# Residual kept token-major: activations stationary, 512 weight columns streamed per load in the FFNs and output projections

## What is computed

```python
for i in range(4):                     # first model; mixers: gated delta, stick-breaking, sparse, gated delta
    x = x + 0.5 * swiglu(rmsnorm(x, ffn1_norm[i]), w_gu, w_down)        # 1024 -> 2 x 2816 -> 1024
    x = x + mixer(rmsnorm(x, mix_norm[i]))                              # ends in h @ w_out, 1024 x 1024
    x = x + 0.5 * swiglu(rmsnorm(x, ffn2_norm[i]), w_gu, w_down)
x = rmsnorm(x, final_norm)
# second model, with gate, shift and scale per feature from a modulation vector
xs + 0.5 * gate * swiglu_2(rmsnorm(xs, g) * (1 + scale) + shift, w_gate, w_up, w_down)   # ctx once, x four times
x + gate * attention(...) ; x + gate * conv(...)                        # one each, both end in @ w_out
rmsnorm(x, final_g)

def rmsnorm(x, g): return x * rsqrt(mean(x * x, -1) + eps) * g
def swiglu(h, ...): return (silu(h @ gate) * (h @ up)) @ down
```

## Time and profile before

| | us |
|---|---|
| median of three runs | 3996.16 |
| range of the runs | 3991.67 to 3997.68 |
| the profiled execution, span | 3996.0 |
| TensorE busy | 3679.5 (92%) |
| VectorE busy | 2434.3 (61%) |
| ScalarE busy | 1783.3 (45%) |
| GpSimd busy | 559.9 (14%) |
| mean granted TensorE clock | 0.954 |

### The profile page before, as it was taken

How to read it: one execution, slowest core, us unless ns; L and a number is a source line. 1 busy time by engine, 2 the same in 40 slices (tenths; PEclk the granted TensorE clock), 3 DMA queues, 4 the chain that set the end, 5 groups by cost and what they waited for, 6 DMA issues and landing times. The chain is left out here.

```text
span 3996.0 us, 67990 instructions
## 1 busy us (share of the span) xinstructions
PE 3679.5 (92%) x28562; PEld 3552.6 (89%) x28562; DVE 2434.3 (61%) x2565; ACT 1783.3 (45%) x2047; POOL 559.9 (14%) x208
## 2 busy tenths in 40 slices
PE   7998788999899998699999789899999889999999
PEld 7997688999899997599999689899999669999999
DVE  4575459797577776677777545554546544545644
ACT  3353255665355554355555234344443344444343
POOL 0001126462032330133310110000001000000000
PEclk9998798999999999899999899999999899999999
DMA  5542045565366663275744015445444215454453
GB/s 206 180 153 79 1 169 210 215 228 200 109 241 235 230 238 115 94 265 211 262 179 169 1 43 190 158 170 178 170 177 166 83 44 194 154 193 158 158 179 126
DMA packets 89670, 652.27 MB, mean 163 GB/s; under 512 B 10000, under 2 KB 10000, under 8 KB 10640
## 3 DMA queue, kind: packets, MB, share of 16 engines
q1 hardware_dynamic: 78480, 572.05, 39.3%
q0 software_dynamic: 11008, 77.60, 5.4%
HBM read 648.56 MB, written 1.05 MB: 163 GB/s over the span
## 5 line engine op out<-in xcount | busy, mean ns | idle before, releaser
L1348 DVE TENSOR_TENSOR w_lo<-raw,w_hi 128x2048 fp32r<-128x2048 f32 x540 | 1390.0, 2580 | 890.0 <-ACT w_hi L909 889.9
L498 PE MATMUL wrk<-h_hi,w_hi 128*128 128x256 f32 x5748 | 1649.5, 287 | 112.7 <-DVE h_lo L1360 68.2
L499 PE MATMUL wrk<-h_hi,w_lo 128*128 128x256 f32 x5748 | 1642.1, 286 | 0.0
L500 PE MATMUL wrk<-h_lo,w_hi 128*128 128x256 f32 x5748 | 1641.2, 286 | 0.0
L909 ACT ACTIVATE w_hi<-raw 128x2048 fp32r<-128x2048 f32 x540 | 1029.9, 1911 | 1047.1 <-PE wrk L500 975.1
L498 PEld LDWEIGHTS wrk<-h_hi,w_hi 128*128 128x128 f32 x5748 | 1120.0, 195 | 125.0 <-issue 118.9
L499 PEld LDWEIGHTS wrk<-h_hi,w_lo 128*128 128x128 f32 x5748 | 1120.3, 195 | 0.4 <-issue 0.2
L500 PEld LDWEIGHTS wrk<-h_lo,w_hi 128*128 128x128 f32 x5748 | 1119.4, 195 | 0.0
L498 PE MATMUL acc<-hid_hi,w_hi 128*128 128x256 f32 x2288 | 652.1, 285 | 21.3 <-DVE w_lo L1348 21.1
L499 PE MATMUL acc<-hid_hi,w_lo 128*128 128x256 f32 x2288 | 650.2, 284 | 0.0
L500 PE MATMUL acc<-hid_lo,w_hi 128*128 128x256 f32 x2288 | 650.1, 284 | 0.0
(11 more groups left out here) (244 smaller groups left out, 3065.5 us busy)
## 6 DMA issues: line engine op xcount, KB each, us to landing
raw<-in_wts SPq DMA_DIRECT2D x540, 1024.0 KB, 4.8
arena<-in_mods POOLq DMA_DIRECT2D x72, 1024.0 KB, 5.1
const<-in_const SPq DMA_DIRECT2D x1, 2176.0 KB, 10.0
c<-in_bias POOLq DMA_DIRECT2D x8, 256.0 KB, 2.9
x<-in_x SPq DMA_DIRECT2D x1, 1024.0 KB, 5.3
c<-in_c SPq DMA_DIRECT2D x1, 1024.0 KB, 5.1
out<-x SPq DMA_DIRECT2D x1, 1024.0 KB, 3.9
vec<-in_vec SPq DMA_DIRECT2D x1, 402.5 KB, 3.2
```

The costliest lines, as they stand in the source:

```text
L498: nc.tensor.matmul(o, wh, rh, start=first, stop=False, skip_group_check=True)
L499: nc.tensor.matmul(o, wl, rh, start=False, stop=False, skip_group_check=True)
L500: return nc.tensor.matmul(o, wh, rl, start=False, stop=last, skip_group_check=True)
L1348: tt(w_lo[:, ns % SLOTS, :], raw[:, ns % SLOTS, :], w_hi[:, ns % SLOTS, :].bitcast(F32), ALU.subtract).then_inc(lo_ready, 1)
```

## The change

The residual becomes token-major (`x`: two halves of 128 tokens on the partitions, 1024 features on the free axis), and so do the results of the FFNs and of the output projections. In those, the activations are now the stationary operand (128 features x 128 tokens) and 512 columns of weights are streamed, which fill a bank. A piece of gate and up holds 512 feature rows of both, 256 columns each. `across` and `along` of the mixers' other projections stay.

- The mean of squares is now a sum along the free axis: ScalarE squares with an accumulator (`statistics`), no matmuls.
- The matmuls still need features on the partitions. TensorE transposes x (16 transposes of 128 x 128 per norm, into `acc`), ScalarE scales and rounds to `h_hi` (`turned_high`), VectorE takes the difference (`turned_low`); with a shift it is two operations per chunk. In a late FFN x is turned unnormalised, and `rstd` is a column that goes into the Silu and into the product.
- `hid` comes out token-major, so each step transposes it (four transposes) before it is split.
- Where the next operation is a late FFN (`follower`), two of its four groups of transposes stand between the last matmuls of the operation before.
- The gate of the second model was a column per partition; it is now a row. Seven operations build it with eight small matmuls (`gate_rows`) and multiply with it in an operation of its own.
- Output projections take the inner dimension in halves, the FFN order on TensorE is rewritten, the loops are unrolled, and the closing norms' gains are loaded as rows.

```diff
+                def gate_up(s, p, t):
+                    n = ns + (3 * s - 1 if s else 0) + p
+                    pe.wait_ge(lo_ready, n + 1)
+                    if s == 0:
+                        pe.wait_ge(n_lo_ready, turned_bank(i, t, p))
+                    u = use[name, f"gu{s}{t}"]
+                    o = bank(u) if p == 0 else wrk[:, u % BANKS, :]
+                    for q in range(4):
+                        k, w = 4 * p + q, slice(q * NB, (q + 1) * NB)
+                        m = products(o, h_hi[:, k, tok(t)], h_lo[:, k, tok(t)], w_hi[:, n % SLOTS, w], w_lo[:, n % SLOTS, w], k == 0, k == KC - 1)
...
+                def turn_hid(s):
+                    pe.wait_ge(taken, use[name, f"gu{s}1"] + 1)
+                    o = bank(use[name, f"t{s}"])
+                    for j in range(2):
+                        for t in range(2):
+                            m = nc.tensor.transpose(o[:, j * T + t * P:j * T + (t + 1) * P], hid[:, t, j * P:(j + 1) * P], cst("ident"))
...
+                def down(s, t, half):
+                    n, q = ns + (3 * s + 4 if s < STEPS - 1 else 3 * s + 2), s % 2
+                    pe.wait_ge(lo_ready, n + 1)
+                    pe.wait_ge(taken, use[name, f"t{s}"] + 1)
+                    for j in range(2):
+                        w = slice(j * D + half * NB, j * D + (half + 1) * NB)
+                        m = products(acc[:, 2 * t + half, :], hid_hi[:, q, j, tok(t)], hid_lo[:, q, j, tok(t)],
+                                     w_hi[:, n % SLOTS, w], w_lo[:, n % SLOTS, w], s == 0 and j == 0, s == STEPS - 1 and j == 1)
...
+                for s in range(1, STEPS):
+                    gate_up(s, 0, 0)
+                    gate_up(s, 0, 1)
+                    turn_hid(s - 1)
+                    gate_up(s, 1, 0)
+                    gate_up(s, 1, 1)
+                    down(s - 1, 0, 0)
+                    down(s - 1, 0, 1)
+                    if s == STEPS - 1:
+                        turn_hid(s)
+                    down(s - 1, 1, 0)
+                    down(s - 1, 1, 1)
+                nxt = follower(i)
+                down(STEPS - 1, 0, 0)
+                down(STEPS - 1, 0, 1)
+                if nxt:
+                    turn(nxt, 0, 0)
+                down(STEPS - 1, 1, 0)
+                if nxt:
+                    turn(nxt, 0, 1)
+                down(STEPS - 1, 1, 1)
...
+            def statistics(i, nth=0, src=None):
...
+                    steps.link(fn(h_tok[:, t, :], xs[:, t, :], ACT.Square, accum_out=stat[:, t:t + 1]))
+                    steps.link(fn(stat[:, t:t + 1], stat[:, t:t + 1], ACT.Ln, scale=1.0 / D, bias=EPS))
+                    fn(stat[:, 2 + t:3 + t], stat[:, t:t + 1], ACT.Exp, scale=-0.5).then_inc(rstd_ready, 1)
...
+            def turned_low(i, t, half, nth=0, prm=None):
...
+                for b in range(4):
+                    k = 4 * half + b
+                    v, o = acc[:, 2 * t + half, b * P:(b + 1) * P], shifted[:, b, :] if shifts else h_lo[:, k, tok(t)]
+                    m = stt(o, v, scale_cols(prm, k)[0], h_hi[:, k, tok(t)].bitcast(F32), ALU.mult, ALU.subtract)
...
             def ffn(i, name, prm):
...
+                if scaled:
+                    for t, half in ((0, 0), (0, 1), (1, 0)):
+                        turned_low(i, t, half)
+                    split_to(ns + 1)
+                    turned_low(i, 1, 1)
                     split_to(ns + 2)
...
                 else:
-                    split_to(ns + 1)
-                    normed(i, prm)
+                    normalise(i)
+                    split_to(ns)
+                    turned_low_all(i)
                     split_to(ns + 2)
...
+            def opening(i):
+                ns = starts[i]["ns"]
+                normalise(i)
+                split_to(ns + 1)
+                turned_low_all(i)
+                split_to(ns + 2)
```

More of the change, by code:

```diff
@@ L408, in mods_before, with late, follower, turned_bank @@
             return sum(len(mod_jobs(name)) for _, name, _ in ops[:i] if name in MOD_OPS)
-        def h_writes(h0):
-            return h0 - KC * sum(k in ("sb", "dsa", "attn") and before(i + 1, "h") <= h0 for i, (k, _, _) in enumerate(ops))
+        def late(kind, prm):
+            return kind == "ffn" and "a" in prm
+        def follower(i):
+            j = i + 1
+            while j < len(ops) and not TURNS[ops[j][0]]:
+                j += 1
+            ok = j < len(ops) and late(ops[j][0], ops[j][2]) and all(k not in UPDATES for k, _, _ in ops[i + 1:j])
+            return j if ok and ops[j][2]["x"] == ops[i][2]["x"] else None
+        def turned_bank(i, t, half, nth=0):
+            return 4 * (before(i, "turn") + nth) + 2 * t + half + 1
+        def tok(t):
+            return slice(t * P, (t + 1) * P)
         def stream(i):
@@ L477, in _ @@
             sp.dma_start(c[:], c_d[:]).then_inc(c_loaded, 16)
[L478 to L481, removed]
+            end = starts[len(ops) - 2]["ns"] + 6
+            load_all(ahead, end)
+            sp.wait_ge(x_new, before(len(ops) - 2, "x"))
+            sp.dma_start(last_row, rows_d[:, 1, :]).then_inc(row_loaded, 16)
+            load_all(end, total["ns"])
+            sp.wait_ge(x_new, before(len(ops), "x"))
+            sp.dma_start(out[:], x[:]).then_inc(stored, 16)
             sp.wait_ge(stored, 16)
@@ new lines, in _, with turn @@
+            turned_early = set()
+            def turn(i, t, half, nth=0, src=None):
+                if (i, t, half, nth) in turned_early:
+                    return
+                turned_early.add((i, t, half, nth))
+                kind, _, prm = ops[i]
+                if late(kind, prm):
+                    if before(i, "x"):
+                        pe.wait_ge(x_new, before(i, "x") - 3 + 2 * t + half)
+                    v = x
+                else:
+                    pe.wait_ge(xn_ready, before(i, "xn") + 2 * nth + t + 1)
+                    v = h_tok
+                if nth:
+                    pe.wait_ge(n_lo_ready, turned_bank(i, t, half))
+                o = acc[:, 2 * t + half, :]
+                for b in range(4):
+                    k = 4 * half + b
+                    m = nc.tensor.transpose(o[:, b * P:(b + 1) * P], v[:, t, k * P:(k + 1) * P], cst("ident"))
+                m.then_inc(turned, 1)
@@ L1437, in ffn @@
-                step(1, static)
-                step(2, static)
-                n_in, per = steps.n, 2 if late else 0
-                with dve.Fori(0, (STEPS - 3) // 2) as r:
-                    steps.at = lambda a: r * per + a
-                    for st in (3, 4):
-                        step(st, lambda a, k: r * k + a)
-                assert steps.n == n_in + per
-                steps.at = lambda a: a
-                steps.n += per * ((STEPS - 3) // 2 - 1)
-                done[0] = ns + 3 * STEPS
```

795 lines of the change are left out of this document (389 added, 406 removed).

## The result

The changed kernel takes 3886.8 us (median of four runs, 3883.2 to 3887.4); in the same comparison the kernel before took 3996.6 (four runs, 3991.7 to 3997.7). The ratio is 0.9729, with an interval of 0.9715 to 0.9743. The forecast was 3786, in a range of 3740 to 3870. The direction was right; the gain is 110 us where 210 were forecast, and the time lies outside the range. The profiled execution has a span of 3885.0 us, so, as before, nothing lies around it.

What follows compares the result with a forecast made beforehand. TensorE, 92% busy, was taken as the bound, with some 95% of each FFN at the matmuls' pace. Terms -134 - 15 - 46 - 19 + 7 - 3 = -210 took 3996 to 3786 us, range 3740 to 3870.

Steps and rivals of the forecast that it cites:

- What 512 columns per load cost: All 10,872 widened matmuls: 0.216 us each, bounds 0.213 and 0.227; streaming 2609.3 to 2348.4 us, 260.9 less.
- rival A: Widened matmuls: the 13 ns are paid per load-and-matmul pair whatever its length, 116 us back, 3902 us; chance 0.10.
- Plain late FFNs: Five late FFNs without modulation: 998.3 to 902.5 us, 180.5 each with a 1 us stall, entry 3.5 us.
- Beside GpSimd: First two FFNs sharing time with GpSimd products: 228.7 to 209 us (VectorE and GpSimd in turn) and 207.3 to 188.
- Turning: Hidden tile in every FFN: 572 transposes of 0.11 us in line on TensorE, 63 us more, nothing waiting.
- D: FFN steps: the chain gate, product, transpose, split becomes the bound; 4215 us with 6.5 us extra latency; chance 0.03.
- E: FFNs: something else, such as the weights, paces them and hides the gain; 3990 us; chance 0.03.
- Entry with modulation: Start of four modulated FFNs: no cheaper, 12 to 12.5 us where 10.2 are now; FFNs 800.3 to 754, 46 less.
- Mixers: Six mixers: later first projections add 3.3 to 7.4 us each, output projections give back 5 and 13.8; sum +7.
- Rival F: 512-column matmuls take 131 ns by the Trainium skill, DMA then limits the steps; about 3220 us; chance 0.01.
- B: New entries and FFNs beside GpSimd stall more, 60 us in all, about 3846 us; chance 0.16.
- C: Entries cheaper than laid out, 3 us in each of 13 FFNs, 3747 us; chance 0.10.

Runs made afterwards that it cites:

- The test on their entry: Version with reordered modulated-FFN entries, plus the mixers' second weight split moved behind the four transpose groups; 3852.7 us, against 3860.2 without the mixer move.
- the streams: Separate kernel without the model, only streams of 32 back-to-back matmuls with weight loads, by width and format; 512 columns: 0.227 us in fp32r, 0.216 in bf16.
- an expected 8 us: Changed kernel with a late FFN's early transposes all moved after the previous operation's last down matmul; 3895.2 us, 8 more.
- the other order: Changed kernel with modulated FFNs' fourth transpose group ahead of the first gate matmuls and second weight split ahead of VectorE's fourth group; 3860.2 us, again 3860.1.

## Why the prediction was wrong in size and right in direction

**The step that failed** is in "What 512 columns per load cost": "I take 0.216 for 512 columns". It is 0.227. The term of the sum was mis-sized by 10,872 x 0.0107 = 116 us: 10,872 x 0.227 = 2468 in place of 2348, so streaming saves 141 us and not 261. This was the upper of the two bounds that the text gave, and rival A, with a time of 3902 and a chance of only 0.10. The range left it out, though it was one of two readings of the same rows.

Why those rows misled: the norm's sum is plain f32, and the matmuls of the kernel are fp32r. At the same stream length the first has 2.7 ns between matmuls and the second 13.3. And the earlier trace rows was read as "the 13 ns vanish behind a stream of 213 ns", but that row has two differences to the earlier trace rows, a longer stream and half the clock. The changed kernel's own 512-column rows part them: at half clock nothing is added to 427 ns, at full clock 13.3 ns are added to 213. It is the clock that made them vanish, not the length, and so the conclusion "the load chain is what is slow at 256 columns, and it disappears behind a longer stream" falls too. No row of before had fp32r at full clock with another width than 256, so the choice between the bounds should have been near even, and the range have gone to 3902.

**The rest of the sum**, by stretches (us). The fourth column puts 0.0107 us on each of the 512-column matmuls of the forecast.

| part | before | after | change forecast | with 0.227 | measured |
|---|---|---|---|---|---|
| first FFN | 222.5 | 215.0 | -15 | -6.6 | -7.5 |
| seven late FFNs | 1437.8 | 1348.2 | -134 | -75 | -89.6 |
| context FFN | 215.0 | 207.8 | -19 | -10.6 | -7.2 |
| four modulated FFNs | 800.3 | 791.8 | -46 | -12 | -8.5 |
| six mixers | 1308.5 | 1313.1 | +7 | +13 | +4.6 |
| end | 11.9 | 9.3 | -3 | -3 | -2.6 |
| sum | 3996.0 | 3885.2 | -210 | -94 | -111 |

- Plain late FFNs: 180.5 forecast, 189 with the true pace; measured 191.1, 187.9, 189.6, 187.9 and 186.5. The entry was laid out rightly to 2 us.
- Beside GpSimd: the first was put at 209, with a bound by VectorE and GpSimd together; 214.2 measured from 3.5 us earlier, so 210.7 by my own stretch. The second: 188 forecast, 196.5 with the true pace, 191.1 measured. These two are most of the 15 us by which the late FFNs beat the corrected sum.
- Turning: 0.11 each and in line, hardly a wait behind it (9.4 us for `hid_lo` in the kernel). The mechanism is right and the 63 us were 51; rivals D and E fell with it.
- Entry with modulation: the sum was right to 4 us, but by luck. The layout gave 12 to 12.5 us on top of the matmuls; measured are 195.6 - 184.6 = 11.0 where the clock stays up and 16.0 where it falls. I saw VectorE's four groups ahead of the second split; I did not see that the last transposes are queued behind the first gate group, nor that the clock costs another 5 us in two of the four.
- Context FFN: 3.4 us more than the corrected sum. Its entry has such pauses too (the second is 3.32 us), and a granted clock of 0.78 from 2493 to 2510 us; it is 1.00 from there on.
- Mixers: I had charged 1.5 us for each more than they lost. The test on their entry shows why that kind of charge is unsafe: what starts earlier there ends no earlier. And their sum is 1313.1 us in one execution of the changed kernel and 1316.0 in another, so 3 us of it mean nothing.
- Rival F (0.131 us per matmul) fell. Nothing near the 60 us of B or the 39 of C is left to explain.
- The 182 GB/s that the text takes from the earlier trace rows isn't there; nothing in the sum hangs on it.

## What to carry to other kernels

The pace of a matmul has to be taken from a row of the same format at the same granted clock; a row that differs in two things can't say which of them matters, and then both bounds belong in the range with nearly equal chances. Each matmul that a wider one makes needless saves 13.3 ns in fp32r and 2.7 in bf16. For the 10,872 saved here that is 145 us and 29 us; against the 51 us that turning costs here the same rewrite in bf16 would not pay. This is an estimate from the streams: no bf16 version of the kernel was run, and transposes in bf16 were not measured. After such a change look at the entries: what one engine has queued ahead of the thing another one waits for was worth another 0.7% here, and part of that was the clock. And where a small effect is expected at one place, look for it at that place: an expected 8 us came as forecast, and the stretches show them elsewhere.

## What was not expected of the hardware

- fp32r at full clock: 0.120, 0.173 and 0.227 us for 256, 384 and 512 columns, a constant 13.3 ns on top of the columns; the same with one stationary tile and with accumulation in one bank. With 128 columns 0.111.
- fp32r at half clock: 0.213 and 0.427 for 256 and 512 columns, nothing on top.
- bf16: 0.056, 0.109 and 0.216 for 128, 256 and 512; plain f32 0.112 and 0.216 per record for 128 and 256, two records to a matmul.
- At the modulated entries a pause of 2.06 us was followed by nine matmuls at half clock in one FFN and by none in another of the same execution; after a pause of 3.29 us fifteen ran at half clock, after one of 2.39 none, and after 1.63 and 1.15 us in the other order none.
